# The last down projection computed with seven half-size products

## The reference

```python
def conv_glu_ffn(xn, w_up, conv_w, conv_b, w_down):
    h = xn @ w_up                       # 512 x 1024 @ 1024 x 5632
    ...                                 # causal conv of width 3 over positions
    gate, up = jnp.split(hc, 2, axis=-1)
    return (jax.nn.silu(gate) * up) @ w_down      # 512 x 2816 @ 2816 x 1024

for l in range(2):
    h = h + hybrid_mixer(rmsnorm(h, norm1_g[l]), ...)
    h = h + conv_glu_ffn(rmsnorm(h, norm2_g[l]), w_up[l], conv_w[l], conv_b[l], w_down[l])
return rmsnorm(h, final_g)
```

## Time and profile before

| | |
|---|---|
| median of 3 runs | 1467.76 us |
| span of the profiled execution | 1465.1 us |
| median minus span | 2.7 us |
| TensorE busy | 1456.5 us, 99% |
| VectorE busy | 964.0 us, 66% |
| ScalarE busy | 671.7 us, 46% |
| GpSimd busy | 45.8 us, 3% |
| TensorE's granted clock, mean | 0.999 |

### The profile page before, as it was taken

One profiled execution on the slowest core, in us unless ns is written; L12 is line 12 of the kernel. 1 busy time (PEld: TensorE's weight loads), 2 busy tenths in 40 slices (PEclk: granted clock), 3 DMA queues, 4 the chain that ended last, 5 costly groups with the idle time before them and its releaser, 6 DMA issues.

```text
span 1465.1 us, 19634 instructions
## 1 busy us (share of the span) xinstructions
PE 1456.5 (99%) x7055; PEld 1205.3 (82%) x7055; DVE 964.0 (66%) x1625; ACT 671.7 (46%) x1153; POOL 45.8 (3%) x34
## 2 busy tenths in 40 slices
PE   9999999999999999999999999999999999999998
PEld 7888888888888888888888888888888888888886
DVE  7877667655787734776477776665658776357753
ACT  8655555443544422343474555544344443234434
POOL 0000000002100000000200000000030000000001
PEclk9999999999999999999999999999999999999999
DMA  6322222232333233322432222222323322332331
GB/s 249 92 68 92 82 59 86 73 104 83 116 100 100 75 98 115 97 86 79 129 128 87 78 82 66 73 87 76 117 89 101 97 90 82 105 111 90 100 106 67
DMA packets 43673, 139.67 MB, mean 95 GB/s; under 512 B 5824, under 2 KB 5952, under 8 KB 43344
## 3 DMA queue, kind: packets, MB, share of 16 engines
q1 hardware_dynamic: 43024, 137.73, 29.8%
q10 hardware_dynamic: 576, 0.97, 0.2%
HBM read 136.52 MB, written 2.10 MB: 95 GB/s over the span
## 4 chain that ended last, share of the span: by engine, by line
PE 96%; DVE 2%; ACT 1%; issue 0%; DMA 0%; DVEq 0%; ACTq 0%
PE dense L655 28%; PE dense L656 28%; PE dense L657 28%; PE turned L738 2%; PE branch L765 1%; PE dense L925 1%; PE dense L927 1%; PE dense L926 1%; PE dense L670 1%; PE dense L672 1%; PE dense L671 1%; PE scores L730 1%; PE scores L727 1%; PE branch L751 1%; ACT tmp L1163 0%
## 5 line engine op out<-in xcount | busy, mean ns | idle before, releaser
L655 PE MATMUL dense<-hg,whi 128*128 128x512 f32 x1304 | 515.7, 395 | 0.2
L657 PE MATMUL dense<-hg,wlo 128*128 128x512 f32 x1304 | 508.3, 390 | 0.0
L656 PE MATMUL dense<-hg,whi 128*128 128x512 f32 x1304 | 507.9, 390 | 0.0
L1009 ACT ACTIVATE whi<-raw 128x1024 fp32r<-128x1024 f32 (+3 forms) x268 | 264.3, 986 | 435.1 <-PE dense L657 408.5
L1362 DVE TENSOR_TENSOR wlo<-raw,whi 128x1024 fp32r<-128x1024 f32 (+3 forms) x268 | 304.7, 1137 | 194.7 <-ACT whi L1009 192.9
L655 PEld LDWEIGHTS dense<-hg,whi 128*128 128x128 f32 x1304 | 245.4, 188 | 52.1 <-DVE wlo L1362 2.6
L657 PEld LDWEIGHTS dense<-hg,wlo 128*128 128x128 f32 x1304 | 244.8, 188 | 52.1
L656 PEld LDWEIGHTS dense<-hg,whi 128*128 128x128 f32 x1304 | 245.1, 188 | 48.2 <-issue 0.2
L655 PE MATMUL dense<-act,whi 128*128 128x512 f32 x528 | 207.2, 392 | 0.0
L657 PE MATMUL dense<-act,wlo 128*128 128x512 f32 x528 | 205.6, 389 | 0.0
L656 PE MATMUL dense<-act,whi 128*128 128x512 f32 x528 | 205.5, 389 | 0.0
(11 more groups left out here) (221 smaller groups left out, 1361.0 us busy)
## 6 DMA issues: line engine op xcount, KB each, us to landing
raw<-in_w_up SPq DMA_DIRECT2D x88, 512.0 KB, 3.5
raw<-in_w_gate SPq DMA_DIRECT2D x48, 512.0 KB, 3.5
raw<-in_w_in SPq DMA_DIRECT2D x26, 512.0 KB, 3.5
raw<-in_w_down SPq DMA_DIRECT2D x32, 384.0 KB, 3.0
raw<-in_w_out SPq DMA_DIRECT2D x16, 512.0 KB, 3.5
raw<-in_w_down SPq DMA_DIRECT2D x16, 320.0 KB, 2.9
raw<-in_w_down_last SPq DMA_DIRECT2D x10, 512.0 KB, 3.5
raw<-in_w_v SPq DMA_DIRECT2D x8, 512.0 KB, 3.5
```

The costliest lines, as they stand in the source:

```text
L655: mm(out, a, xhi, start=start, stop=False)
L656: mm(out, a, xlo, start=False, stop=False)
L657: return mm(out, b, xhi, start=False, stop=stop)
L1009: fn(whi[:, s, 0:cols], raw[:, r, 0:cols], ACT.Copy).then_inc(w_hi.sem, 1)
```

## The change

The last layer's feed-forward block is no longer cut into halves: the up projection of all 22 pairs comes first, then the whole down projection. That is one product A (512 positions x 2816) times B (2816 x 1024). The scheme of Strassen (in Winograd's form, with shared sums) is applied to it with A cut in two over positions and in two over hidden chunks (even chunks, odd chunks), and B in two over hidden chunks and in two over output columns. Seven products of half size in each direction stand for eight. `KP` = 11 is the number of chunk pairs.

- The sum over the 11 pairs is run twice, as 22 steps `q_`. In the first pass each step does the products p1, p5, p6, p4, in the second p7, p2, p3. Each product is 2 tiles of 128 positions x 3 matmuls of 512 columns. In the first pass the eight PSUM banks hold the four products; in the second six of them hold three.
- The sums of blocks of B are done by GpSimd after the weights have landed: three subtractions of 512 columns per step in the first pass (`first_sums`), one in the second. The sums of blocks of A are done by GpSimd too: two of 256 columns per pair after the GLU (`activation_sums`), and one of 512 columns per step in the second pass (`second_sums`).
- Only then are the operands split into high and low. So in the last layer `gated` and `gated_lo` no longer split the GLU's output, which VectorE writes as float32 (`x_raw`). Per step of the first pass ScalarE copies and VectorE subtracts 1024, 512, 256, 1024 and 256 columns (`SPLITS_1`); in the second 512, 512, 1024 and 256 (`SPLITS_2`).
- Weights come as 1 MB per step in the first pass and 768 KB in the second, into three buffers; one of these, and the second set of split operands, lie in `hg`, which is free after the up projection. SyncE issues a load when step q - 3 has been split.
- The folds of the products into the result (`fold_in`) are VectorE's: `FOLDS` between the passes, `LATE_FOLDS` two per step in steps 12 to 16, `END_FOLDS` at the end. ScalarE first copies p1 out of PSUM.
- The residual is turned during the first two pairs of the up projection. The final norm goes tile by tile in the order 2, 3, 0, 1; GpSimd's product with the gain row comes with it.

```diff
 HALVES = (12, 10)
-LAST_GROUPS = HALVES[1] // 2
-LAST_UNITS = 2 * LAST_GROUPS
+KP = FF // 2
+FIRST_PASS, SECOND_PASS = ("p1", "p5", "p6", "p4"), ("p7", "p2", "p3")
+FIRST_ENDS = ("p1", "p6", "p5", "p4")
 NEG = -1e30
...
+Q_A11, Q_S2, Q_A12, Q_A22 = range(4)
+H2 = S // 2
+LAST_W = {"p1": 0, "p5": S, "p6": 2 * S, "p4": 3 * S, "p2": 0, "p3": S, "p7": 2 * S}
+LAST_X = {"p1": 0, "p6": H2, "p5": 2 * H2, "p4": 3 * H2, "p3": 0, "p7": H2, "p2": 2 * H2}
+SPLITS_1 = ("w01", "x01", "x2", "w23", "x3")
+SPLITS_2 = ("w2", "x01", "w01", "x2")
+NEEDS = {"p1": "x01", "p5": "x2", "p6": "w23", "p4": "x3", "p7": "x01", "p2": "x2", "p3": "x2"}
...
+def order_of(q):
+    return SECOND_PASS if q >= KP else FIRST_ENDS if q == KP - 1 else FIRST_PASS
+
+
...
+FOLDS = [("u", 0), ("u", 1), ("v", 0), ("v", 1)]
+LATE_FOLDS = [("w", 0), ("w", 1), ("u21", 0), ("u21", 1), ("v12", 0), ("v12", 1), ("v22", 0), ("v22", 1), ("p4", 0), ("p4", 1)]
+END_FOLDS = [("p7l", 0), ("p7r", 0), ("p7l", 1), ("p7r", 1), ("p2", 0), ("p2", 1), ("p3", 0), ("p3", 1), ("p3h", 1)]
...
+        x_raw = act2_f[:, 0:FF * S].rearrange("p (c s) -> p c s", s=S)
+        q_flat = q[:, :, :].rearrange("p c s -> p (c s)")
+        hg_flat = hg[:, :, :, :].rearrange("p i c s -> p (i c s)")
+        raw_flat = raw[:, :, :].rearrange("p r n -> p (r n)")
+        w_ops = [[whi[:, :, :].rearrange("p s n -> p (s n)"), wlo[:, :, :].rearrange("p s n -> p (s n)")],
+                 [hg_flat[:, 0:4 * S], hg_flat[:, 4 * S:8 * S]]]
+        x_ops = [[probT_r[:, 0:2 * S], probT_r[:, 2 * S:4 * S]], [hg_flat[:, 8 * S:10 * S], hg_flat[:, 10 * S:12 * S]]]
+        raw_last = [raw_flat[:, 0:4 * S], raw_flat[:, 4 * S:8 * S], hg_f[:, 12 * S:16 * S]]
+
+        def x_quarter(p, i, n=1):
+            return act2_f[:, (4 * p + i) * H2:(4 * p + i + n) * H2]
+
+        def s1_of(p):
+            return act2_f[:, FF * S + p * H2:FF * S + (p + 1) * H2] if p < 4 else q_flat[:, 8 * S - (KP - p) * H2:8 * S - (KP - p - 1) * H2]
+
+        w_sum, v_sum = [k[:, t, :] for t in range(2)], [k[:, 2 + t, :] for t in range(2)]
+        u_sum = [v[:, t].rearrange("p t d -> p (t d)") for t in range(2)]
+
         bank = [ps(f"dense{i}") for i in range(NBANK)]
         bank_s = [ps("scores0"), ps("scores1")]
         bank_t = ps("turned")
         bank_y = ps("branch")
         bank_r = [bank_s[0], bank_s[1], bank_t, bank_y]
+        junk_r = tmp[1][:, :]
+        bank_of = {"p1": bank_s, "p5": [bank_t, bank_y], "p6": bank[0:2], "p4": bank[2:4],
+                   "p7": bank_s, "p2": [bank_t, bank_y], "p3": bank[0:2]}
...
+                for q_ in range(2 * KP):
+                    if q_ < 2:
+                        sp.wait_ge(w_lo.sem, w_lo.at(l, NMIX + NUP - 3 + 2 * q_))
+                    elif q_ == 2:
+                        sp.wait_ge(used.sem, used.at(l, NMIX + NUP - 1))
+                    else:
+                        sp.wait_ge(last_l, split_at(q_ - 3, "w23" if q_ - 3 < KP else "w01"))
+                    src = A["w_last1"][q_] if q_ < KP else A["w_last2"][q_ - KP]
+                    sp.dma_start(raw_last[q_ % 3][:, 0:4 * S if q_ < KP else 3 * S], src).then_inc(last_in[q_ % 3], 16)
+                    if q_ == KP:
                         sp.dma_start(gain_row, A["gain_row"]).then_inc(gain_row_in, 16)
...
+            def tile(q_, x, t, start, stop, to=None, cols=slice(0, S)):
+                at = LAST_W[x]
+                a, b = [w_ops[q_ % 2][i][:, at + cols.start:at + cols.stop] for i in range(2)]
+                at = LAST_X[x] + t * P
+                x_hi, x_lo = [x_ops[q_ % 2][i][:, at:at + P] for i in range(2)]
+                to = bank_of[x][t][:, cols] if to is None else to
+                mm(to, x_hi, a, start=start, stop=False)
+                mm(to, x_hi, b, start=False, stop=False)
+                return mm(to, x_lo, a, start=False, stop=stop)
...
+                for q_ in range(2 * KP - 2):
+                    for x in order_of(q_):
+                        pe.wait_ge(last_l, split_at(q_, NEEDS[x]))
+                        if q_ == 0 and x == "p1":
+                            pe.wait_ge(fin_res, 2 * T)
+                        if q_ == 0 and x in ("p6", "p4"):
+                            pe.wait_ge(hp.sem, hp.at(l, NUP - 3 if x == "p6" else NUP - 1))
+                        for t in range(2):
+                            if q_ == KP and x == "p7":
+                                pe.wait_ge(copied, t + 1)
+                            elif q_ == KP:
+                                pe.wait_ge(fold, FOLD_AT[("v" if x == "p2" else "u", t)])
+                            last = tile(q_, x, t, q_ in (0, KP), q_ == KP - 1)
+                            if q_ == KP - 1 and t == 0:
+                                last.then_inc(tile_a, 1)
+                        last.then_inc(last_p, 1)
+                ends = (2 * KP - 2, 2 * KP - 1)
+                for x in SECOND_PASS[0:2]:
+                    for t in range(2):
+                        for q_ in ends:
+                            pe.wait_ge(last_l, split_at(q_, NEEDS[x]))
+                            last = tile(q_, x, t, False, q_ == ends[1])
+                        last.then_inc(tile_b, 1)
+                for q_ in ends:
+                    last = tile(q_, "p3", 0, False, q_ == ends[1])
+                last.then_inc(tile_b, 1)
+                tile(ends[0], "p3", 1, False, False)
+                tile(ends[1], "p3", 1, False, True, cols=slice(0, 2 * P)).then_inc(tile_b, 1)
+                pe.wait_ge(fold, FOLD_AT[("p4", 1)])
+                tile(ends[1], "p3", 1, True, True, to=bank[2][:, 0:2 * P], cols=slice(2 * P, S)).then_inc(tile_b, 1)
...
+            def last_hi(l, q_, what):
+
+                first = q_ < KP
+                s, r = q_ % 2, raw_last[q_ % 3]
+                if q_ >= 2:
+                    x = {"w01": "p5", "x01": "p6", "x2": "p5", "w23": "p4", "x3": "p4"}[what] if q_ < KP else order_of(q_ - 2)[-1]
+                    act.wait_ge(last_p, product_at(q_ - 2, x))
+                elif what[0] == "w":
+                    act.wait_ge(used.sem, used.at(l, NMIX + NUP - (2 if (q_, what) == (0, "w01") else 1)))
+                elif q_ == 1:
+                    act.wait_ge(used.sem, used.at(l, NMIX + NUP - 1))
+                if what[0] == "w":
+                    act.wait_ge(last_in[q_ % 3], 16 * (q_ // 3 + 1))
+                    act.wait_ge(w_sums, 3 * q_ + (1 if what == "w01" else 3) if first else 3 * KP + q_ - KP + 1)
+                elif first and what != "x3":
+                    act.wait_ge(pair_sum, 2 * q_ + 2)
+                elif first:
+                    act.wait_ge(glu.sem, glu.at(l, 2 * q_ + 1))
+                elif what == "x01":
+                    act.wait_ge(x_sums, q_ - KP + 1)
+                fn(last_to(q_, what, 0), last_from(q_, what), ACT.Copy).then_inc(last_h, 1)
...
+            def last_lo(q_, what):
+                dve.wait_ge(last_h, split_at(q_, what))
+                ve.tensor_tensor(last_to(q_, what, 1), last_from(q_, what), last_to(q_, what, 0).bitcast(F32),
+                                 ALU.subtract).then_inc(last_l, 1)
...
+                late = list(LATE_FOLDS)
+                for q_ in range(2 * KP):
+                    for what in splits_of(q_):
+                        last_lo(q_, what)
+                        if (q_, what) == (0, "x2"):
+                            taps(l, 0, 0, last, 1)
+                            hp_evac(l, 0, 1, last, 1)
+                    if q_ == 1:
+                        gated(l, 0, last, 1)
+                    if q_ == KP:
+                        for x, t in FOLDS:
+                            fold_in(x, t)
+                    if q_ > KP:
+                        for x, t in late[0:2]:
+                            fold_in(x, t)
+                        late = late[2:]
 
             def halve_gate_bias(l):
...
+            def activation_sums(l, p):
+                pool.wait_ge(glu.sem, glu.at(l, 2 * p + 1))
+                nc.gpsimd.tensor_tensor(s1_of(p), x_quarter(p, Q_S2), x_quarter(p, Q_A22), ALU.add).then_inc(pair_sum, 1)
+                pool.wait_ge(pair_sum, 2 * p + 1)
+                nc.gpsimd.tensor_tensor(x_quarter(p, Q_S2), s1_of(p), x_quarter(p, Q_A11), ALU.subtract).then_inc(pair_sum, 1)
+
+            def first_sums(q_):
+                b11, t1, t2, t4 = [raw_last[q_ % 3][:, i * S:(i + 1) * S] for i in range(4)]
+                pool.wait_ge(last_in[q_ % 3], 16 * (q_ // 3 + 1))
+                nc.gpsimd.tensor_tensor(t1, t1, b11, ALU.subtract).then_inc(w_sums, 1)
+                pool.wait_ge(w_sums, 3 * q_ + 1)
+                nc.gpsimd.tensor_tensor(t2, t2, t1, ALU.subtract).then_inc(w_sums, 1)
+                pool.wait_ge(w_sums, 3 * q_ + 2)
+                nc.gpsimd.tensor_tensor(t4, t2, t4, ALU.subtract).then_inc(w_sums, 1)
+
+            def second_sums(q_):
+                p = q_ - KP
+                b22, t3 = [raw_last[q_ % 3][:, i * S:(i + 1) * S] for i in (1, 2)]
```

(28 more changed lines are left out.)

360 lines of the change are left out of this document (186 added, 174 removed).

## The result

The changed kernel takes 1491.01 us (1490.59 to 1493.59, four runs) against 1467.68 us (1467.6 to 1468.1, four runs) of the kernel before beside it: ratio 1.0163, interval 1.0148 to 1.0177. It is 23.3 us slower. The execution that was profiled took 1493.59 us, 2.0 above its span, so it lies at the upper end of the runs.

What follows compares the result with a forecast made beforehand. TensorE bounds the old kernel; in the new down projection VectorE's and GpSimd's added held times would. -15.0 (matmuls) + 33.6 (waiting) + 2 (end) = +20.6 on the 1465.1 us span, plus 2.7 around it: 1488 us, range 1476 to 1501.

Steps and rivals of the forecast that it cites:

- the first case: Down projection's splits: held times of VectorE and GpSimd add up, supply bounds both passes; 1488 us, 79%.
- 66 matmuls fewer, 15.0 us: TensorE, down projection: 462 matmuls instead of 528, 0.227 us each, 15.0 us saved; steps need 5.45 and 4.09 us.
- DMA and ScalarE hidden: First-pass steps: 1 MB lands in 5 to 6 us, ScalarE's copies take 3.5 of 5.45 us; neither costs time.
- They don't run side by side: VectorE's two-SBUF-input operations and GpSimd's sums exclude each other, holding 1.07 (1024 columns) and 1.15 us (512).
- The sum, 131 us to step 21's `x01`: From last up matmul to that split: held times total 125.4 to 136.9 us, 131 taken; TensorE waits 33.6 us.
- The signs: Steps at 6.7 to 7.3, then 4.7 to 5.2 us; 1024-column splits well over 1.23, GpSimd's sums near 1.9 to 2.2.
- 33 matmuls, 7.5 us: After step 21's `x01` split TensorE has 33 matmuls left, 7.5 us, ending at 138.5 instead of 104.9.
- The end, 2 us (0 to 4): Tail: VectorE has 10.2 us of work against TensorE's 7.5, and GpSimd's gain products block it; 2 us lost.
- The up projection, zero: Up projection: VectorE's slack covers GpSimd's two sums per pair; no change, bounds 0 and +1 us.
- No exclusion: Splits of each step: sums fall into VectorE's idle time, TensorE stays the bound; -10.6 us, 1457, 7%.
- The late chain: Load, three dependent sums, copy, split with three buffers are late, nothing overlapped; +14 us on top, 1502, 10%.
- The falling clock: TensorE's idle gaps lower the clock to 1.2 GHz: whole first pass +44, 1532; few us after step 2, +5; 4%.

Runs made afterwards that it cites:

- experiment 1: Changed kernel with each of GpSimd's 55 down-projection sums replaced by a zero fill that reads nothing, same waits and signals, operands unsummed: 1460.65 us, ratio 0.9948.
- experiment 2: Changed kernel without the 55 GpSimd sums at all, only bare semaphore signals in their place, operands unsummed: 1460.23 us, ratio 0.9945.
- experiment 3: Changed kernel with a second, useless GpSimd addition of 512 columns behind each of the 55 sums: 1536.01 us, ratio 1.0461.
- experiment 9: Changed kernel with GpSimd's gain-row products at the tail replaced by fills with ones: 1492.02 us, ratio 1.0163; run again, 1489.57 us beside the changed kernel's 1493.21.
- experiment 7: Changed kernel with sums beside the down projection on VectorE, step 2 loaded early, some sums on GpSimd during the up projection, other reordering: 1466.25 us, ratio 0.9987.
- experiment 8: Kernel of experiment 7 with step 2's sums earlier, step 1's on VectorE, last GLU later, one more sum ahead, last gain products held back: 1462.10 us, ratio 0.9962.
- experiment 5: Changed kernel with only the first pass's sums of steps 2 to 10 on VectorE; GpSimd keeps steps 0, 1 and the second pass: 1481.44 us, ratio 1.009.
- experiment 6: Changed kernel with the sums of steps 2 to 21 on VectorE, plus one useless GpSimd sum in each of steps 4 to 9: 1475.19 us, one run.

## Why the prediction was right

The forecast was the first case, that both lists add up, at 1488 us. It came to 1491.01. By its steps:

- **66 matmuls fewer, 15.0 us.** Held. Where operands are ready, steps come at 5.44 and 4.08 us (experiment 1) for 5.45 and 4.09 said. The page counts 69 fewer, because some records are missing.
- **DMA and ScalarE hidden.** ScalarE fills 68.75 of 142.3 us, yes. 1 MB landed in 4.7 us (5 to 6 said). But GpSimd waited for loads for about 36 us in the stage. It was no bound: without the exclusion waits remained (25 us of the stage in experiment 1) and the steps still came at TensorE's pace. It made GpSimd's sums fall thinner in some places, and the turns with it.
- **They don't run side by side.** Held, and it is nearly all of the loss: experiments 1 and 2 give back 30 us, experiment 3 takes 45 for 55 more. The held times from the earlier trace rows (1.07, 1.15) are those of the down projection (1.09, 1.14, 1.15, 1.08).
- **The sum, 131 us to step 21's `x01`.** Its low part ended 134.4 us after zero, inside the 125.4 to 136.9 and 3.4 over what I took. At first sight the passes are off in different directions: the first pass's splits were done at 79.0 where its lists add up to 70.5 to 76.7, and the rest took 55.4 (54.9 to 60.2). GpSimd's timeline clears it up: by then it had done the first four sums of the second pass (at 1409.49, 1410.94, 1413.96 and 1415.22), 4 x 1.15 = 4.6 us of the port. With these counted where they belong it is 74.4, in the middle, and 60.0, at the upper end. So the term mis-sized is the second pass: I took the low end "in the steps where both always have work", by held times, and it came near what the lone paces add up to. The signs say the same. Steps 1 to 9 come at 7.1 us on average (6.7 to 7.3 said), but they scatter from 5.5 to 9.0; steps 11 to 19 come at 5.3 (4.7 to 5.2 said). And the median of the low parts of 1024 columns, said to be well over 1.23, is 1.22, since only 14 of 32 met a sum; that of GpSimd's sums of 512 columns is about 1.6, not 1.9 to 2.2.
- **33 matmuls, 7.5 us.** 7.9 (1481.3 less 1473.5, rounded). So TensorE waited for 37.4 us where 33.6 were said.
- **The end, 2 us (0 to 4).** It was 3.7: the last fold starts 5.1 us after the last matmul does, before 1.1. Two of VectorE's products stood for 1.81 and 1.67 instead of 0.75, together 2.0 us, so the blocking was priced right. In the profiles of experiment 9 the tail is 2.0 us shorter, and 1.7 remain. VectorE's list is longer than TensorE's there, which I had worked out (10.2 against 7.5) but not added.
- **The up projection, zero.** TensorE fills 238.17 of 238.20 us. Held.

**The rivals.** No exclusion (1457, the other side): false as a mechanism, but experiment 1 measures it, 1460.65; the sum for it was 3.6 too low. By experiment 1's profile some 2 of these are at the tail again (4.0 for 2 said) and 1 in the first steps (2.1 for 1 said). The late chain (1502): refuted by experiment 1, in which the chain is whole. The falling clock (1532, or +5): partly true. The granted clock is 0.95 over the stage. Right after waits of TensorE of 2.0 to 2.3 us it stood at the 1.2 GHz level for some us, at four places (from 1349.9, 1374.3, 1417.8 and 1441.6). The first two (columns as in the stretches above):

```profile
1350.00:1354.00 4.00, 4.00 (x11) 3.18 (x12) 3.93 (x7) 2.62 (x4) 0.00 (x0) 0.57 0.43 113
1374.00:1378.00 4.00, 3.75 (x10) 2.98 (x11) 4.00 (x4) 1.13 (x2) 3.84 (x3) 0.57 0.00 0
```

In the first stretch eleven matmuls start in 4 us, 0.36 us each instead of 0.227: about 1.5 us of TensorE's time. It cost little, since TensorE would have waited for VectorE otherwise; VectorE was idle for 2.7 of 142.3 us in all, which bounds what the clock and everything else can have taken from it. How much of the 2.7 is the clock's is open.

In sum the profiled span is 5.9 us over the 1485.7 forecast: 3.8 more waiting, 1.7 more at the tail, 0.4 ahead of zero. The median is only 2.6 over its 1488.4. That it comes so near is in part luck: the execution profiled lies 2.6 above the median, and 2.0 us lie around its span where I added 2.7.

## What to carry to other kernels

Before work is moved to an idle GpSimd, look what VectorE is doing at that time: if it works on two inputs from SBUF, and the two engines take turns, the moved operations cost VectorE their whole held time (here 1.15 us for 512 columns of float32), and doing them on VectorE (0.67) is cheaper. An engine's idle share says nothing about a port that it shares; add the lists of both. GpSimd's free time is usable where VectorE has slack, or for operations that only write; here doing the sums on VectorE turned 1491 into 1472.5 us, and moving some of them ahead into the up projection, with the other moves of experiments 7 and 8, made it 1462.

## What the runs showed of the hardware

- **Turns, or starvation.** In the changed kernel the two engines alternate operation by operation. In experiments 5 and 6 a GpSimd sum that came while VectorE ran such operations back to back is shown as 7.34 and 40.42 us: it ended 1.15 us after VectorE's train did in the one, and only once VectorE had an operation out of PSUM in the other. VectorE lost nothing. The Trainium skill (SBUF — State Buffer, "Who interferes with whom") says that whoever issues first has the port for the instruction and the other blocks. The turns agree with it; a wait over many instructions stands beside them in these traces. What decides between the two I haven't found: the arrival within VectorE's operation looks alike in the earlier trace rows, where the turn came at once, and in experiment 6.
- **What one operation holds.** A sum of 512 columns of float32 on GpSimd held 1.15 us; the useless one of experiment 3, which adds a tile to itself, 0.90 (21 times between 1359 and 1430); VectorE's low parts 1.08 for 1024 columns, 0.54 for 512, 0.28 for 256.
- **A writing operation isn't blocked.** GpSimd's memset of 1408 columns took 1.28 us beside VectorE's 1.22, neither longer for the other.
- **The clock fell after short waits.** In the changed kernel the four stretches at the lower level follow waits of TensorE of 2.0 to 2.3 us. But a wait does not settle it: after another of 2.25 us (to 1365.26) the granted clock was 1.00, and so it was in experiment 5 after one of 2.88 (to 1356.47). In experiments 1 and 2 no wait of the stage is longer than 1.4 us, and the granted clock was 1.00 in it.
